# Latent attention in head pairs: a new order of turns on four engines, and the first scores between the first pair's last norms

## What is computed

```python
kv = (ckv_all @ w_ukv).reshape(B, S, MLA_HEADS, MLA_NOPE + MLA_V)
k_nope = rms_norm(kv[..., :MLA_NOPE], kn_nope)
v = kv[..., MLA_NOPE:]
q = (rms_norm(cq_raw, q_norm) @ w_uq).reshape(B, T, MLA_HEADS, MLA_NOPE + MLA_ROPE)
...
s = einsum('bqhd,bshd->bhqs', q, k) * (q.shape[-1] ** -0.5)
p = softmax(where(k_pos // 64 <= q_pos // 64, s, NEG_BIG))
o = einsum('bhqs,bshd->bqhd', p, v)
```

## Time and profile before

| | us |
|---|---|
| median of 3 executions | 4640.33 (4639.83 to 4645.03) |
| profiled execution, its own time | 4648.07 |
| its span, first to last instruction | 4646.2 |
| mean granted TensorE clock, share of full | 0.973 |

### The profile page before, as it was taken

How to read it: one execution, slowest core, us unless ns; L and a number is a source line. 1 busy time by engine, 2 the same in 40 slices (tenths; PEclk the granted TensorE clock), 3 DMA queues, 4 the chain that set the end, 5 groups by cost and what they waited for, 6 DMA issues and landing times. The chain is left out here.

```text
span 4646.2 us, 74610 instructions
## 1 busy us (share of the span) xinstructions
PE 4293.6 (92%) x29488; PEld 3000.1 (65%) x29488; DVE 2286.2 (49%) x4732; ACT 1638.6 (35%) x3886; POOL 816.4 (18%) x980
## 2 busy tenths in 40 slices
PE   7999998988999989999979999989898999899999
PEld 4665665666666667777446656656666666677774
DVE  3566663455524453534435666634555244535344
ACT  4333433455523342112043334334555243421120
POOL 0011000000010024544300110000000100245443
PEclk9999999999999999999989999999999999999999
DMA  5010012100021122322250110121000211223222
GB/s 202 22 32 16 30 27 84 35 14 16 10 91 54 58 75 88 111 89 69 87 196 23 31 24 22 27 84 35 14 16 11 91 54 58 75 90 108 92 72 83
DMA packets 129148, 280.76 MB, mean 60 GB/s; under 512 B 30041, under 2 KB 55897, under 8 KB 123554
## 3 DMA queue, kind: packets, MB, share of 16 engines
q1 hardware_dynamic: 128802, 275.99, 17.8%
HBM read 230.96 MB, written 42.62 MB: 59 GB/s over the span
## 5 line engine op out<-in xcount | busy, mean ns | idle before, releaser
L1063 PE MATMUL banks<-hT,w_piece 128*128 128x384 f32 x1536 | 536.7, 491 | 0.2
L1063 PEld LDWEIGHTS banks<-hT,w_piece 128*128 128x128 f32 x1536 | 276.3, 190 | 161.3 <-issue 6.7
L2246 PE MATMUL banks<-hT,w_piece 128*128 128x384 f32 x1056 | 354.1, 489 | 1.5 <-ACT sb_gate_raw L2356 1.5
L2246 PEld LDWEIGHTS banks<-hT,w_piece 128*128 128x128 f32 x1056 | 196.1, 190 | 141.4 <-issue 16.6
L2012 DVE SCALAR_TENSOR_TENSOR keysT<-banks,gains,rstd 64x128 f32<-64x128 f32 (+1 forms) x272 | 112.1, 412 | 246.2 <-ACT rstd L1926 243.7
L2702 DVE TENSOR_TENSOR gate_quarters<-gate_kept,banks 128x288 f32<-128x288 f32 x144 | 65.4, 454 | 298.9 <-PE banks L2565 293.9
L2653 ACT ACTIVATE gate_kept<-banks 128x288 f32<-128x288 f32 x144 | 59.0, 410 | 429.3 <-PE banks L2565 429.3
L2702 DVE TENSOR_TENSOR branch_quarters<-branch_kept,banks 128x288 f32<-128x288 f32 x144 | 65.4, 454 | 268.5 <-PE banks L2565 268.3
L2415 DVE TENSOR_TENSOR pass<-pass,constants 128x128 f32<-128x128 f32 x128 | 41.9, 327 | 311.1 <-ACT take L2367 308.2
L2418 DVE TENSOR_TENSOR_SCAN left<-pass,zero 128x384 f32<-128x384 f32 (+7 forms) x144 | 189.8, 1318 | 5.0
L1023 POOL TENSOR_TENSOR state_decayed<-state,decay_of_chunk 128x128 f32<-128x128 f32 x120 | 85.9, 716 | 531.5 <-DVE state L1301 531.5
(11 more groups left out here) (427 smaller groups left out, 9791.6 us busy)
## 6 DMA issues: line engine op xcount, KB each, us to landing
w_piece<-in_w_cols SPq DMA_DIRECT2D x66, 512.0 KB, 4.3
w_ada<-in_w_ada SPq DMA_DIRECT2D x24, 1024.0 KB, 9.0
w_gate_ahead<-in_w_cols SPq DMA_DIRECT2D x48, 512.0 KB, 4.4
w_branch<-in_w_br SPq DMA_DIRECT2D x96, 256.0 KB, 2.9
w_gate<-in_w_cols SPq DMA_DIRECT2D x48, 512.0 KB, 4.3
y_branch<-y_gated SPq DMA_DIRECT2D x12, 1152.0 KB, 8.8
sb_cached_keysT<-in_sbkT SPq DMA_DIRECT2D x8, 1024.0 KB, 7.6
sb_cached_values<-in_sbv SPq DMA_DIRECT2D x8, 1024.0 KB, 5.2
```

What stands on the lines that cost most here:

```text
L1063: last = mm(dst, w[0 if kind in ("k", "v") else 1][:, k, :], hT[:, k, c], start=(k == 0), stop=(k == KD - 1))
L2246: last = mm(ps[:, bank[n], 0:TG], w_of[wn][:, k, :], hT[:, k, TG * g:TG * g + TG], start=(k == 0), stop=(k == KD - 1))
```

## The change

In the loops, on each engine:

- PE: scores(u + 2), sums of step u - 1, turns(u), raw fills of u, value fills of u, values(u - 1). Norm fill x of the next pair moves one step earlier, to step x - 1, and norms 0 and 1 both stand at step 0.
- ACT: rows(u - 2), roots of step u - 1, columns(u), value copies of u, squares of u, exps(u + 2).
- DVE: normalise(u), maximum(u + 2), norms of step u - 1.
- Value fills of pairs 1 to 3 leave banks 6 and 7 and take a place in the ring (banks 4 and 5), between turns(u) and values(u - 1).

At the start the last six fills of pair 0 use banks 6, 7, 4, 1, 5, 3 rather than 6, 7, 0, 1, 2, 3. PE does scores(0) right behind the last raw fill and scores(1) behind the sums of fill 21, then turns(0) once banks 4 and 5 are free, and goes on once 1 and 3 are. DVE does maximum(0) before norm fill 21, maximum(1) before 22 and normalise(0) before 23; ACT does exps(0) before root 21 and exps(1) before root 22. The diff, without the new semaphores' names and the places where a wait for a value fill is merely reworded:

```diff
@@ -1619,7 +1619,7 @@
         if x % 2 == 1 and x // 2 < len(LA_VALUES):
             fills.append(("value", 0, LA_VALUES[x // 2], -1))
     for h in range(1, HP):
-        steps = [(x, "norm", h, p) for x, p in enumerate(LA_PREP)] + [(v, "value", h, q) for v, q in zip(LA_VALUE_STEPS, LA_VALUES)]
+        steps = [(max(x - 1, 0), "norm", h, p) for x, p in enumerate(LA_PREP)] + [(v, "value", h, q) for v, q in zip(LA_VALUE_STEPS, LA_VALUES)]
         for step, kind, hh, p in sorted(steps, key=lambda e: (e[0], e[1])):
             fills.append((kind, hh, p, NU * (h - 1) + step))
     fills.sort(key=lambda f: (f[3], f[3] >= 0 and f[0]))
@@ -1627,16 +1627,15 @@
     bank, norms = [], []
     for n, (kind, h, p, step) in enumerate(fills):
         if n < START:
-            bank.append((6, 7, 0, 1, 2, 3)[n % 6])
-        elif kind == "norm":
-            bank.append(6 + len(norms) % 2)
+            bank.append((6, 7, 0, 1, 2, 3)[n % 6] if n < 18 else (6, 7, 4, 1, 5, 3)[n - 18])
         else:
-            bank.append(6 + len(norms) % 2)
+            bank.append(6 + len(norms) % 2 if kind == "norm" else None)
         if kind == "norm":
             norms.append(n)
...
+        for n in at_step[u]:
+            if fills[n][0] == "value":
+                ring["v", n] = len(ring)
...
+        def values_made(eng, h, group):
+            n = find["value", h, group]
+            if h == 0:
+                released(eng, n)
+            else:
+                eng.wait_ge(ring_free, ring["v", n] + 1)
...
-                begin(n)
+                if h == 0:
+                    begin(n)
+                else:
+                    take_ring(("v", n))
+                b = bank[n] if h == 0 else ring_bank(("v", n))
...
-                last.then_inc(fill_ready, 1)
+                last.then_inc(fill_ready if h == 0 else ring_ready, 1)
...
+                            for n in range(18):
+                                if bank[n] in (0, 2):
                                     released(pe, n)
...
                     (raw if fills[n][0] == "norm" else value_rows)(n)
                 if 0 <= n - 3 < START and fills[n - 3][0] == "norm":
                     sums(n - 3)
-            scores(0)
-            scores(1)
+                if n in (START - 1, START):
+                    scores(n - START + 1)
+            for n in range(18, START):
+                if bank[n] in (4, 5):
+                    released(pe, n)
+            turns(0)
+            for n in range(18, START):
+                if bank[n] in (1, 3):
+                    released(pe, n)
             for u in range(U + 1):
                 mine = at_step[u]
+                scores(u + 2)
+                if u >= 1:
+                    for n in at_step[u - 1]:
+                        if fills[n][0] == "norm":
+                            sums(n)
+                if 1 <= u < U:
+                    turns(u)
                 for n in mine:
                     if fills[n][0] == "norm":
                         raw(n)
-                scores(u + 2)
-                if u < U:
-                    turns(u)
                 for n in mine:
                     if fills[n][0] == "value":
                         value_rows(n)
                 values(u - 1)
-                for n in mine:
-                    if fills[n][0] == "norm":
-                        sums(n)
...
-                act.wait_ge(fill_ready, n + 1)
+                act.wait_ge(fill_ready, nth_fill[n])
...
+                    act.wait_ge(ring_ready, max(ring["v", n], ring["o", NU * (h - 1) + 2 * last_pair + 1]) + 1)
+                    do(to, ps[:, ring_bank(("v", n)), 0:P * count], Copy).then_inc(ring_free, 1)
...
-            exps(0)
-            exps(1)
+                if n in (START, START + 1):
+                    exps(n - START)
             for u in range(U + 2):
                 mine = at_step[u]
                 rows(u - 2)
-                for n in mine:
-                    if fills[n][0] == "norm":
-                        square(n)
+                if u >= 1:
+                    for n in at_step[u - 1]:
+                        if fills[n][0] == "norm":
+                            root(n)
                 columns(u)
-                exps(u + 2)
                 for n in mine:
                     if fills[n][0] == "value":
                         value_rows(n)
                 for n in mine:
                     if fills[n][0] == "norm":
-                        root(n)
+                        square(n)
+                exps(u + 2)
...
             for n in range(START):
+                if n == START - 3:
+                    maximum(0)
+                elif n == START - 2:
+                    maximum(1)
+                elif n == START - 1:
+                    normalise(0)
                 if fills[n][0] == "norm":
                     norm(n)
-            maximum(0)
-            maximum(1)
             for u in range(U + 2):
-                normalise(u)
-                for n in at_step.get(u - 1, []):
-                    if u >= 1 and fills[n][0] == "norm":
-                        norm(n)
+                if u >= 1:
+                    normalise(u)
                 maximum(u + 2)
+                if u >= 1:
+                    for n in at_step[u - 1]:
+                        if fills[n][0] == "norm":
+                            norm(n)
```

More of the change, by code:

```diff
@@ L1639, in latent_pairs @@
     uses = [bank[:n].count(bank[n]) for n in range(len(fills))]
+    nth_fill = [sum(b is not None for b in bank[:n + 1]) for n in range(len(fills))]
     find = {(f[0], f[1], f[2]): n for n, f in enumerate(fills)}
@@ L1654, in latent_pairs @@
     names = ("once_loaded", "par_loaded", "ahead_loaded", "w0_loaded", "w1_loaded", "qa_loaded", "qb_loaded", "gate0_loaded", "gate1_loaded",
-             "fill_ready", "free0", "free1", "free2", "free3", "free6", "free7", "squared", "summed", "rooted", "spread", "zeroed",
+             "fill_ready", "free0", "free1", "free2", "free3", "free4", "free5", "free6", "free7", "squared", "summed", "rooted", "spread", "zeroed",
              "scores_ready", "max_done", "exps_done", "scaled", "ring_ready", "ring_free", "gated",
@@ L1658, in latent_pairs @@
     with S.stage(*names) as (block, sb, (once_loaded, par_loaded, ahead_loaded, w0_loaded, w1_loaded, qa_loaded, qb_loaded, gate0_loaded, gate1_loaded,
-                                         fill_ready, free0, free1, free2, free3, free6, free7, squared, summed, rooted, spread, zeroed,
+                                         fill_ready, free0, free1, free2, free3, free4, free5, free6, free7, squared, summed, rooted, spread, zeroed,
                                          scores_ready, max_done, exps_done, scaled, ring_ready, ring_free, gated,
                                          y0_stored, y1_stored, y2_stored, vec)):
-        free = {0: free0, 1: free1, 2: free2, 3: free3, 6: free6, 7: free7}
+        free = {0: free0, 1: free1, 2: free2, 3: free3, 4: free4, 5: free5, 6: free6, 7: free7}
         w_loaded, gate_loaded, y_stored = (w0_loaded, w1_loaded), (gate0_loaded, gate1_loaded), (y0_stored, y1_stored, y2_stored)
@@ L1700, in weights @@
                 if h >= 2:
-                    released(sp, find["value", h - 2, LA_VALUES[-1]])
+                    values_made(sp, h - 2, LA_VALUES[-1])
                     released(sp, find["norm", h - 2, LA_PREP[-1]])
@@ L1808, in value_rows @@
                 kind, h, (first, count), step = fills[n]
-                begin(n)
+                if h == 0:
[3 more added lines that the diff above has]
+                b = bank[n] if h == 0 else ring_bank(("v", n))
                 for q in range(count):
                     for k in range(2):
-                        last = mm(ps[:, bank[n], P * q:P * q + P], latT[:, k, P * (first + q):P * (first + q) + P], wkv[h][:, k, P:2 * P],
+                        last = mm(ps[:, b, P * q:P * q + P], latT[:, k, P * (first + q):P * (first + q) + P], wkv[h][:, k, P:2 * P],
                                   start=(k == 0), stop=(k == 1))
-                last.then_inc(fill_ready, 1)
+                last.then_inc(fill_ready if h == 0 else ring_ready, 1)
             def scores(u):
@@ L1828, in scores @@
                             pe.wait_ge(once_loaded, 64)
-                            for n in range(START):
-                                if bank[n] < 4:
+                            for n in range(18):
+                                if bank[n] in (0, 2):
                                     released(pe, n)
@@ L1867, in values @@
                 if kind == "s":
-                    released(pe, find["value", h, LA_VALUES[4]])
+                    values_made(pe, h, LA_VALUES[4])
                     s = slot_no[u, 0] % 4
@@ L1878, in values @@
                     if i == NPT - 1:
-                        released(pe, find["value", h, LA_VALUES[-1]])
+                        values_made(pe, h, LA_VALUES[-1])
```

(11 more changed lines are left out.)

## The result

| | before | after |
|---|---|---|
| median, us | 4640.08 (4630.39 to 4645.03, 4 executions) | 4597.65 (4596.41 to 4599.69, 4 executions) |
| ratio | | 0.991 (95%: 0.9896 to 0.9924) |
| profiled execution, us | 4648.07 | 4598.66 |
| mean granted clock | 0.973 | 0.976 |

The changed kernel is 42.4 us faster by the medians, where 40 was forecast, and 49.4 by the profiled executions. Lines have moved: raw fills are L1802 to L1808, sums L1814, value fills L1825, scores L1847 to L1857, transposes L1869, `values` L1887 to L1895 on PE; squares L1938, roots L1945 and L1947, exponentials L1966 on ACT; norms L2037, maxima L2048 to L2050, normalise L2056 and L2057 on DVE.

The account below looks back on a forecast made before the run. PE, busy 92% of the span, was taken to bound the kernel. A layer gains 25.2 in pairs, less 4.5 at the start and 0.7 for clock; two layers give 40 us, 4640.3 to 4600 us, range 4586 to 4628.

Parts of the forecast that it names:

- pairs -25.2: Layer 0's three windows between scores(k = 4): 267.6 us falls to 82.5, 82.5 and 77.4, gaining 25.2.
- start +4.5: Start of each layer: ACT and DVE take turns, PE idles some 10 us; 3 to 6 us slower, taken as 4.5.
- clock -0.7 taken off: Each layer's gain: 0.7 us taken off for short falls of the clock at new waits.
- The best end of the range: Best case: gains of 8 us a pair and an even start, 2 x 27 = 54 us, 4586 us.
- 8.1 us of idle time and 14 x 0.2: PE's waits in the old full-clock pair: idle time plus 0.2 us for each of 14 waits, 10.9 us lost.
- Value fills in the ring: Loop steps: value fills' waits for DVE go; in wide steps about 0.1 us remains where 0.36 to 0.6 idled.
- The square behind the value copy: On ACT, the square can't pass the value copy, so PE's sums wait for it, 1.8 us in every pair.
- The chain over DVE: Root, norm, normalise hold PE: 1.6 us in step 1, 0.65 in step 14, 1.0 in step 17.
- Rival 1: ACT's queue binds: transposes' copies 0.4 us later in ten wide steps a pair; 4619 us, chance 0.14.
- Rival 2: At the start both engines run ahead, PE goes on 6 us sooner than before; 4579 us, chance 0.05.
- Rival 4: Waits are replaced one for one and nothing moves; 4640 us, chance 0.06.
- Rival 3: New waits of 1.6, 1.0 and 0.65 us in each pair draw long clock falls; 4690 us, chance 0.07.

Follow-up runs that it names:

- old_loop_new_start: The kernel before, its loop kept, given the changed kernel's new start; 4654.11 us, ratio 1.0029.
- values_in_6_7: The changed kernel's order of turns, but value fills of pairs 1 to 3 again in banks 6 and 7; 4629.05 us, ratio 0.9975.
- columns_first: The changed kernel with ACT's copies of the transposes ahead of the roots of step u - 1; 4623.6 us, ratio 0.9962.
- square_first: The changed kernel with ACT's squares of step u ahead of the value copies of step u; 4587.4 us, ratio 0.9886.
- new_loop_old_start: The changed kernel's new loop with the start of the kernel before; 4592.04 us, ratio 0.9896.

## Why the prediction was right

**The sum.** Forecast for a layer: pairs -25.2, start +4.5, clock -0.7 taken off. Measured in the traces: pairs 267.56 to 240.36 in layer 0 and 267.64 to 240.11 in layer 1, -27.2 and -27.5; start +3.9 and +3.4. That is -47.4 for both layers of the 49.4 between the profiled executions; 40 was forecast. The mechanism and each sign were right; the pairs were sized within 0.9 us each (82.5 and 77.4 beside 81.63 to 81.92 and 76.81), the start within 1.1. That the median came so near, 42.4 beside 40, is in part luck: for the profiled execution the same sum gave 4608, and it took 4598.66, 9.4 less. The profiled execution of before lay 7.7 us above its median then, that of after lies 1.0 above its own.

The best end of the range was added up wrongly: 8 us a pair with an even start are 24 us a layer and not 27, so 4592 and not 4586. The pairs alone gained more than that best case.

**What of it is the clock.** Between the cuts each layer of before has two falls of 3.4 us and one of 10.2. A short one costs 1.6 us (old_loop_new_start), so 3.1 a layer. The long one costs about 3.4 by an estimate: the last window of layer 1 holds it alone and takes 87.84 us, where 88.02 less the 3.5 of the fills that it lacks would be 84.5 if the waits were those of the quiet pair. So some 6.5 of a layer's 27 us came with falls that are gone. The prediction took all 2.2 us between 90.18 and 88.02 for a short fall; 0.6 of them are pair 0's without any.

**What waits cost before.** I took 8.1 us of idle time and 14 x 0.2. The kernels' difference of 6.1 us in the quiet pair, with 5.2 left by the starts of groups in the new one, makes it 11.3 and not 10.9: 0.4 short, which is the wait at L1874, 0.2 of idle time and my 0.2 for a wait, that I had left out of the sum.

**Value fills in the ring.** Right, and the largest part: values_in_6_7 gives 5.2 of 6.1 us back in a quiet pair, and 15 of 27 in a layer. The wait of 0.1 that I left for `values` in wide steps isn't there, nor the 0.4 behind value steps. My ACT backlog had each operation at its full row length, but the next one starts before a row ends (in after the copy at 1101.25 has 0.60 us and the square behind it starts 0.50 later). In columns_first the same slack shows from the other side: the root has little of it, the copy has some.

**The square behind the value copy.** The timeline of after in pair 1, from a value fill to the next sums:

```profile
1118.16 1.50 PE L1825 MATMUL banks<-w_ukv,latentT 128*128 128x128 f32 x12
...
1119.50 0.60 PE L1857 MATMUL banks<-keysT,queriesT 96*128 96x256 f32 x2
...
1120.09 0.38 ACT L1938 ACTIVATE squares<-banks 128x256 f32<-128x256 f32 x1
...
1120.52 0.70 PE L1814 MATMUL banks<-squares,constants 128*128 128x256 f32 x2 [0.42 <-ACT squares L1938]
```

The value fill ends its issue at 1119.50, scores two tiles wide follow, the square stands behind the value copy until 1120.09, and the sums start at 1120.52, 1.02 us after that end, 0.42 of them idle. I had 1.15 to 1.2, and 0.6 of it uncovered at this width. From start to start the four such waits in narrow steps lose 0.16, 0.38, 0.48 and 0.31 us, 1.3 beside my 1.8; square_first gained 1.8, as the start of each group behind a wait is slower too. The square's raw fill was long done, and it still stood behind the copy. By the rule of the Trainium skill, "PSUM — Partial Sum Buffer", section "Engine vs sequencer instructions", that ScalarE's queue is strictly first in, first out, it has to; the trace agrees.

**The chain over DVE.** Forecast 1.6 in step 1, 0.65 in step 14, 1.0 in step 17; measured from start to start in pair 1 of layer 0 2.0, 0.8 and 1.0. All three stand where they were put. Step 1 is under-sized in this pair alone: at the five other places PE idles 1.59 us, as forecast, and DVE goes from maximum(k = 3) into norm 0 without a pause; here DVE idles 0.33 us between them, PE 1.88, and the pair is 0.3 longer. What DVE waited for there isn't settled.

**The start.** The step-by-step count from the square to scores(2) gave 15.43 us behind the last raw fill (957.87 to 973.3); 15.42 is what every kernel shows that has that start and the new loop. The turns of ACT and DVE are its terms one by one: norm 19 to maximum(0) 1.47, maximum 1.11, exponentials 0.58, root 1.01. The loss at the lower clock I took as about 4 us; scores(k = 4) came 27.5 and 27.2 us after the raw fill where the forecast has 28.3. It was over-sized by about 1: of the 13.7 us of the low stretch 6.3 and 6.9 still lay in the 9.6 of idle time.

**The rivals.** Rival 1 (the copies late by 0.4 us) falls: no such wait is left. Rival 2 (the start fills the idle time) falls by old_loop_new_start and new_loop_old_start. Rival 4 falls with the result. Rival 3 needed new waits to draw falls of the clock, and waits of that length do stand ahead of falls in these traces. In the old loop (before and old_loop_new_start) a fall of 3.4 us begins within 1 us of the end of six of twelve waits of 1.9 us, and a fall of 10.2 begins within each of the four waits of 2.0 us ahead of the last pair's first wide score. In columns_first three of six waits of 2.5 to 2.8 us have a fall of 3.4 at their end, and a fourth fall stands behind waits of 0.35 and 1.20. But behind the 42 waits of 1.6 to 1.9 us of the seven other profiled executions with the new loop there is none. So the rival falls here because the new order's waits drew no fall, and not because such waits can't. The prediction's sentence that only the 10 us wait at the start pays, which would make the rival void, isn't borne out. What sets one wait of 1.9 us apart from another isn't settled.

## What to carry to other kernels

A hand-written order on an in-order engine is a list of who may hold whom: before moving a step, name what stands behind it on its own engine and what that waits for. Two edits of this change were both meant to spare PE idle time. The one that gave two kinds of fill banks of their own paid 5 us a pair, and the one that broke DVE's and ACT's runs into a chain of turns cost 3.4 to 3.9 a layer in all, most of it by that chain. Where PE must idle, put into that time what has no one waiting in front of it, such as the next raw fills, and leave the engines that set the end of the wait their unbroken run.

## What the runs showed of the hardware

The granted clock's lower level (1.2 GHz) began within PE's idle time at the start in every kernel, and how long it lasted differed. It was 13.7 us behind 9.6 us of idle time (ten layers of five profiled executions and both of old_loop_new_start), 10.2 behind 5.5 to 6.3 in five layers, and 6.8 in the two layers where the idle time was 3.8 and 4.0. The kernel before has the exception: behind the same 6.1 us it lasted 10.2 in layer 0 and 13.7 in layer 1, so the idle time alone doesn't set it. At the head of the stage, behind a wait of 2.7 us, a fall of 3.4 to 6.8 us came in some executions and layers and not in others of the same instructions (none in layer 1 of after, 6.8 us in its layer 0), worth 1.5 to 3 us. And the same pair of one kernel with the same waits took 89.59 us with a fall of 3.4 us and 88.02 without, so that a gain read from one pair of one profile can be 1.6 us off by that alone.
